# A recurrent head's output read by two engines, a weight piece behind the turned keys, mask rows on the weight queue

## The chip, the core and the metric

The kernel runs on one core of a Trainium2 chip. The metric is the device time of one execution in microseconds: 2011.34 us is the median of three runs before the change, which lay between 2010.67 and 2016.43 us.

## The reference

One inference step of a two-layer encoder. Its tokens are 16 meta tokens and 512 prompt frames of a new stream, and 8 running streams of 16 frames: 656 in all. Each layer mixes tokens in two head groups side by side, eight heads of latent attention and four recurrent heads (HGRN2), and then has a gated channel mixer. The change touches the recurrent heads and the start of the attention behind them:

```python
def hgrn_chunk(S, q, gl, k, v):
    G = jnp.cumsum(gl, axis=1)
    o_inter = jnp.einsum('bthk,bhkv->bthv', q * jnp.exp(G), S)
    A = jnp.einsum('bthk,btshk,bshk->bhts', q, decay, k)
    o = o_inter + jnp.einsum('bhts,bshv->bthv', A, v)
    S_new = jnp.exp(G_last)[..., None] * S + jnp.einsum('bshk,bshv->bhkv', k * jnp.exp(G_last[:, None] - G), v)
    return S_new, o
...
    o = rmsnorm(o, gain) * jax.nn.silu(hg.astype(f32).reshape(B, T, HG_HEADS, HG_DV))
```

## The kernel before

All data lies with features on the partitions and the 656 tokens along the row. Each engine has one program, written out in order; semaphores tie them together. Weights come as 512 KB pieces of 128 x 1024 numbers. SP loads piece g into one of two raw buffers (`wraw`) once piece g - 2 is split; ACT rounds it to its high part (`whi`, in `w_high`), DVE takes the rest (`wlo`, in `w_low`), and TensorE multiplies with both. SP's loop over the pieces issues them strictly in this order, with other transfers between them at fixed places.

The four recurrent heads of a layer run one after the other (`for h in range(HG)` on each engine). TensorE fills the gaps of head h with the input tiles of the next head, or, in the last head, with the query tiles of the attention (`fill`). Within a head:

- Eight levels (`level`, DVE's `hg_diff`, `hg_decayed`, `hg_take`, ACT's `exp_level`) build the masked products A of queries and keys, with two banks of the PSUM tensor WA in turn.
- `turns`: TensorE turns the values into WA and the keys into WB. ACT copies them to `vtok`, `Z` and `ktok`. Before that ACT has the gates of the next head, then one `w_high`.
- `state_sums`: TensorE multiplies turned keys and values. DVE then builds the running states `st` from WA (`state`), and `dec`.
- `head_out`: TensorE makes the head's output in WA, 512 prompt columns in the first bank, 16 meta and 128 sample columns in the second, and signals `o`.
- ACT squares the output for its norm (`sq`), and DVE multiplies it by gain and gate into `ob` and signals `o_taken`. POOL multiplies the old state S by `dec` (`decay_state`). `new_state` and `finish` on DVE come within the next head.
- TensorE waits for `o_taken` before level 0 of the next head, which writes into WA again; behind the last head it waits for it before `keys(0)`.

Behind the last head of a layer come the key tiles (`keys(0)` to `keys(3)`, copied by ACT to KT in `take_keys`), the sum of squares of the last head, and the first scores (`prompt_scores(l, 0)`). These need three transfers, the mask rows: `kpe` copied to rows 64 to 96 of KT for eight heads (528 KB), and four rows each for KT and Y. They wait for `o` and `dec` of the last head, since KT and Y overlay what that head still reads.

In the profile L420 is TensorE's `mm`, L424 its transposes, L950 ACT's `activation`, L1416 DVE's helper, L364 POOL's `decay_state`, L371 POOL's sum of a rotated query tile (`add_rotated`), L331 the load of a weight piece; L1147, L1149, L1150 are the mask rows and L1151 the state's way out.

## Time and profile before

| | us |
|---|---|
| median of three runs | 2011.34 |
| lowest and highest run | 2010.67, 2016.43 |
| the profiled execution | 2010.24 |
| its span in the trace | 2008.4 |
| TensorE busy in it | 1902.1 |
| DVE busy | 1129.7 |
| ACT busy | 761.2 |
| POOL busy | 115.4 |

The span runs from the first to the last instruction of the trace. Busy times overlap, so only the engine that others wait for counts. Views of the trace name an instruction as out<-in with the kernel's own tensor names, with the idle time before it and what ended that idle time. The granted clock of TensorE is given as a share of 2.4 GHz: 1.00 in most stretches and 0.5, that is 1.2 GHz, in some.

### The profile page before, as it was taken

What the parts mean: (1) busy time and instruction counts of PE and PEld (TensorE: products, weight loads), DVE (VectorE), ACT (ScalarE), POOL (GpSimd) and SP (SyncE); (2) the same over time, 40 slices, a digit from 0 to 9 for tenths busy, and PEclk for the clock granted to TensorE, in tenths of its full rate; (3) what the DMA queues carried; (4) which work ended last, traced back from release to release, by engine and by line L of the source; (5) the groups of instructions that cost most, each with busy time, mean ns of one, the idle gap of its engine ahead of it and who ended that gap; (6) DMA issues with size and microseconds to landing.
All of it is one profiled execution on the core that took longest, in us unless ns stands there. A gap on an engine that the chain in (4) does not pass through costs nothing.

```text
span 2008.4 us, 30210 instructions
## 1 busy us (share of the span) xinstructions
PE 1902.1 (95%) x12028; PEld 1741.8 (87%) x12028; DVE 1129.7 (56%) x1807; ACT 761.2 (38%) x1207; POOL 115.4 (6%) x117
## 2 busy tenths in 40 slices
PE   7999989999999999999999998899999999999996
PEld 6988875579899999999888898655889999999994
DVE  5677775534776316663467778544257662366535
ACT  5434545434432222223453444454354222222235
POOL 0000033300000000000000001332000000000000
PEclk9999999999999999999999999899999999999998
DMA  5111121222121222222121111204112222222211
GB/s 185 66 55 55 65 61 38 78 85 74 51 85 69 76 72 74 74 74 74 55 97 44 55 63 54 85 3 139 57 53 67 77 71 75 73 74 74 74 64 58
DMA packets 45116, 141.82 MB, mean 71 GB/s; under 512 B 5472, under 2 KB 11488, under 8 KB 44960
## 3 DMA queue, kind: packets, MB, share of 16 engines
q1 hardware_dynamic: 36704, 120.20, 17.3%
q10 hardware_dynamic: 8272, 19.69, 3.0%
q8 instruction: 96, 1.57, 0.3%
q14 instruction: 44, 0.36, 0.1%
HBM read 130.13 MB, written 8.65 MB: 69 GB/s over the span
## 4 chain that ended last, share of the span: by engine, by line
PE 72%; DVE 14%; ACT 10%; issue 2%; ACTq 1%; DMA 1%; DVEq 0%; SPq 0%
PE G L420 60%; PE WA L420 7%; PE WB L420 3%; DVE wlo L1416 2%; DVE tmp L1416 2%; DVE Y L1416 1%; ACT Y L950 1%; ACT sq L950 1%; DVE DE L1416 1%; ACT whi L950 1%; PE G L424 1%; DVE X L1416 1%; PE WB L424 1%; DVE Z L1416 1%; ACT Hh L950 1%
## 5 line engine op out<-in xcount | busy, mean ns | idle before, releaser
L420 PE MATMUL G<-Hh,wlo 128*128 128x328 f32 x2144 | 690.5, 322 | 30.4 <-DVE Hl L1416 27.6
L420 PE MATMUL G<-Hh,whi 128*128 128x328 f32 x2144 | 675.6, 315 | 0.0
L420 PE MATMUL G<-Hl,whi 128*128 128x328 f32 x2144 | 670.0, 312 | 0.0
L420 PEld LDWEIGHTS G<-Hh,wlo 128*128 128x128 f32 x2144 | 407.4, 190 | 46.6 <-DVE Hl L1416 32.7
L420 PEld LDWEIGHTS G<-Hh,whi 128*128 128x128 f32 x2144 | 406.9, 190 | 1.6 <-issue 0.2
L420 PEld LDWEIGHTS G<-Hl,whi 128*128 128x128 f32 x2144 | 406.7, 190 | 0.0
L950 ACT ACTIVATE whi<-wraw 128x1024 fp32r<-128x1024 f32 x192 | 203.6, 1060 | 515.6 <-PE G L420 490.9
L1416 DVE TENSOR_TENSOR wlo<-wraw,whi 128x1024 fp32r<-128x1024 f32 x192 | 236.4, 1231 | 237.5 <-ACT whi L950 227.6
L420 PE MATMUL G<-gl,whi 128*128 128x328 f32 x704 | 220.4, 313 | 0.0
L420 PE MATMUL G<-gh,wlo 128*128 128x328 f32 x704 | 220.2, 313 | 0.0
L420 PE MATMUL G<-gh,whi 128*128 128x328 f32 x704 | 219.6, 312 | 0.0
L420 PEld LDWEIGHTS G<-gh,whi 128*128 128x128 f32 x704 | 132.2, 188 | 0.2
L420 PEld LDWEIGHTS G<-gh,wlo 128*128 128x128 f32 x704 | 132.2, 188 | 0.2
L420 PEld LDWEIGHTS G<-gl,whi 128*128 128x128 f32 x704 | 132.2, 188 | 0.0
L1416 DVE TENSOR_TENSOR ax<-G,R 128x328 f32<-128x328 f32 (+2 forms) x126 | 48.6, 386 | 136.5 <-PE G L420 133.2
L950 ACT ACTIVATE tmp<-cc 128x528 f32<-128x528 f32 x88 | 42.3, 480 | 145.3 <-DVE cc L1416 143.9
L420 PEld LDWEIGHTS WA<-Z 128*128 128x128 f32 x576 | 71.6, 196 | 27.3 <-DVE Z L1416 16.6
L420 PE MATMUL WA<-Z 128*128 128x64 f32 (+1 forms) x576 | 73.3, 274 | 18.5 <-DVE Z L1416 10.5
L1416 DVE SCALAR_TENSOR_TENSOR cc<-ax,cols,cc 128x672 f32<-128x672 f32 x88 | 80.9, 919 | 3.1
L364 POOL TENSOR_TENSOR S<-S,dec 128x1024 f32<-128x1024 f32 x8 | 15.2, 1897 | 1039.5 <-PE WA L420 1039.3
L950 ACT ACTIVATE DE<-DE 128x512 f32<-128x512 f32 (+1 forms) x64 | 45.3, 708 | 66.3 <-DVE DE L1416 62.8
L1416 DVE TENSOR_TENSOR DE<-Y 128x328 f32<-128x328 f32 (+4 forms) x136 | 61.7, 454 | 5.1
(243 smaller groups left out, 2429.5 us busy)
## 6 DMA issues: line engine op xcount, KB each, us to landing
wraw<-in_wstream SPq DMA_DIRECT2D x192, 512.0 KB, 3.2
ckT<-in_ckT SPq DMA_DIRECT2D x12, 512.0 KB, 3.9
ctok<-in_ctok SPq DMA_DIRECT2D x12, 512.0 KB, 3.3
S<-in_s ACTq DMA_DIRECT2D x8, 512.0 KB, 6.0
o_sst<-S ACTq DMA_DIRECT2D x8, 512.0 KB, 3.1
o_y<-Y SPq DMA_DIRECT2D x16, 164.0 KB, 1.8
ckT<-in_ckT ACTq DMA_DIRECT2D x4, 512.0 KB, 3.9
ctok<-in_ctok ACTq DMA_DIRECT2D x4, 512.0 KB, 3.8
```

What stands on the lines that cost most here:

```text
L364: pool.tensor_tensor(s3, s3, dec[:, :].rearrange("p (b a) -> p b a", a=1).broadcast_to([P, DB, P]), ALU.mult).then_inc(S("s0_decayed"), 1)
L420: return pe.matmul(out, lhsT, rhs, start=start, stop=stop, skip_group_check=True)
L424: return pe.transpose(out, in_, ident[0:n, 0:n])
L950: return act.activation(*args, **kw)
L1416: return kind(*args, **kw)
```

## The change

Three edits, in both layers:

1. In each head, ACT's `w_high` of the piece that stood before the copy of the turned values now stands behind that of the turned keys, and DVE's `w_low` of this piece stands behind `dec` instead of before the state updates.
2. ACT squares the 512 prompt columns of the output and signals `sq_prompt`; meanwhile DVE multiplies the 16 and 128 columns of the second bank and signals `ob_side`. Then ACT squares these, and DVE multiplies the 512. Before, DVE's three products waited for all three squares. TensorE waits for the last squares on its own before `keys(0)`.
3. The three mask-row transfers move from ACT's queue to SP's, just before weight piece 26 of the layer (`P_OUT + 4`), with the same two waits.

```diff
--- before.py
+++ after.py
@@ -326,6 +326,15 @@
                             latents(l, b + 1)
                         sp.wait_ge(S("s_oa"), l * DB + b - 1)
                         sp.dma_start(ctok[:, b % 2, :], a["ctok"][l, b]).then_inc(S(f"ct_in{b % 2}"), 16)
+                if g % PIECES == P_OUT + 4:
+
+                    l = g // PIECES
+                    sp.wait_ge(S("o"), HG * (l + 1))
+                    sp.wait_ge(S("dec"), HG * (l + 1))
+                    sp.dma_start(KT[64:96, :, :], kpe[64:96, 0:PT].rearrange("p (a n) -> p a n", a=1)
+                                 .broadcast_to([ROPE, HM, PT])).then_inc(S("maskrows"), 16)
+                    sp.dma_start(KT[96:100, :, :], a["krows"]).then_inc(S("maskrows"), 16)
+                    sp.dma_start(Y[96:100, :, :], a["qrows"]).then_inc(S("maskrows"), 16)
                 if g >= RAW:
                     sp.wait_ge(S("w_split"), g - RAW + 1)
                 sp.dma_start(wraw[:, g % RAW, :], a["wstream"][g // PIECES, stored(g % PIECES)])\
@@ -824,6 +833,7 @@
                     mm(WB[0:P if i < 4 else META, c:c + 512], kvn[:, cs], wA[:, 512:1024]).then_inc(S("values"), 1)
 
                 pe.wait_ge(S("o_taken"), l * HG + HG)
+                pe.wait_ge(S("sq"), squares(n0 + N_HG[HG - 1]) + 1)
                 keys(0)
                 keys(1)
                 pe.wait_ge(S("s0_new"), l * HG + HG)
@@ -1122,11 +1132,9 @@
                     did(f(DE[:, 0, :], DE[:, 0, :], ACT.Exp), "E")
                     if not end:
                         gates(h + 1)
-                        w_high(l, SPL + 8 + 4 * h)
                     else:
                         for q in range(HG):
                             q_nope(q)
-                        w_high(l, SPL + P_UQ)
                     act.wait_ge(S("v_turned"), n + 1)
                     did(f(vtok[:, 0:640], WA[:, 0:640], ACT.Copy), "act")
                     did(f(vtok[0:META, 640:768], WA[0:META, 640:768], ACT.Copy), "act")
@@ -1136,23 +1144,19 @@
                     act.wait_ge(S("k_turned"), n + 1)
                     did(f(ktok[:, 0:640], WB[:, 0:640], ACT.Copy), "act")
                     did(f(ktok[0:META, 640:768], WB[0:META, 640:768], ACT.Copy), "tok")
+                    w_high(l, SPL + 8 + 4 * h if not end else SPL + P_UQ)
                     if not end:
                         exp_level(h + 1, 0)
                     else:
                         q_nope(4)
                         q_nope(5)
                     act.wait_ge(S("o"), n + 1)
-                    if end:
-                        act.wait_ge(S("dec"), n + 1)
-                        act.dma_start(KT[64:96, :, :], kpe[64:96, 0:PT].rearrange("p (a n) -> p a n", a=1)
-                                      .broadcast_to([ROPE, HM, PT])).then_inc(S("maskrows"), 16)
-                        act.dma_start(KT[96:100, :, :], a["krows"]).then_inc(S("maskrows"), 16)
-                        act.dma_start(Y[96:100, :, :], a["qrows"]).then_inc(S("maskrows"), 16)
                     act.dma_start(a["o_pst"][l, h], st[:, 4, :]).then_inc(S("pst_out"), 16)
                     c = squares(n0 + N_HG[h])
                     if c >= 2:
                         act.wait_ge(S(sq_free(c)[0]), sq_free(c)[1])
-                    did(f(sq[:, c % 2, META:PT], WA[:, 0:512], ACT.Square), "act")
+                    did(f(sq[:, c % 2, META:PT], WA[:, 0:512], ACT.Square), "sq_prompt")
+                    act.wait_ge(S("ob_side"), n + 1)
                     did(f(sq[:, c % 2, 0:META], WA[:, 512:512 + META], ACT.Square), "act")
                     did(f(sq[:, c % 2, PT:T], WA[:, 640:640 + SAMP], ACT.Square), "sq")
 
@@ -1617,7 +1621,7 @@
                     did(tt_(ob[:, h, :], ob[:, h, :], R2[:, :], ALU.mult), "ob")
                     did(mark(), "R2_used")
 
-                def take_tile(h, u):
+                def take_tile(h, u, split=True):
 
                     i = 6 + 4 * h + u
                     to = (hq(h + 1), gate[:, (h + 1) % 2, :], hv(h), hk(h))[u] if i < T_LAT else \
@@ -1630,7 +1634,8 @@
                         did(mark(), "R_used")
                     else:
                         scaled(t0 + i, to)
-                    w_low(l, SPL + i)
+                    if split:
+                        w_low(l, SPL + i)
 
                 gated(0)
                 hg_diff(l, 0, 0)
@@ -1686,11 +1691,10 @@
                         gated(h + 1)
                         hg_diff(l, h + 1, 0)
                         dve.wait_ge(S("v_turned"), n + 1)
-                        take_tile(h, 2)
+                        take_tile(h, 2, False)
                     else:
                         queries(2)
                         queries(3)
-                        w_low(l, SPL + P_UQ)
 
                     dve.wait_ge(S("dS"), n + 1)
                     if n:
@@ -1703,19 +1707,21 @@
                     if n:
                         dve.wait_ge(S("s0_decayed"), n)
                     did(cp(dec[:, :].rearrange("p (b a) -> p b a", a=1), samples(DE[:, 1, PT:T])[:, :, DT - 1:DT]), "dec")
+                    w_low(l, SPL + 8 + 4 * h if not end else SPL + P_UQ)
                     if not end:
                         hg_decayed(l, h + 1, 0)
                     else:
                         queries(4)
                         queries(5)
 
-                    c = squares(n0 + N_HG[h])
+                    def gated_out(to, src):
+                        return stt(ob[:, h, to], src, col(l, C_HGN), gate[:, h % 2, to], ALU.mult, ALU.mult)
+
                     dve.wait_ge(S("o"), n + 1)
-                    dve.wait_ge(S("sq"), c + 1)
-                    gt = gate[:, h % 2, :]
-                    for (p0, p1), (a0, a1) in (((0, 512), (META, PT)), ((512, 512 + META), (0, META))):
-                        step(stt(ob[:, h, a0:a1], WA[:, p0:p1], col(l, C_HGN), gt[:, a0:a1], ALU.mult, ALU.mult))
-                    did(stt(ob[:, h, PT:T], WA[:, 640:640 + SAMP], col(l, C_HGN), gt[:, PT:T], ALU.mult, ALU.mult), "o_taken")
+                    step(gated_out(slice(0, META), WA[:, 512:512 + META]))
+                    did(gated_out(slice(PT, T), WA[:, 640:640 + SAMP]), "ob_side")
+                    dve.wait_ge(S("sq_prompt"), n + 1)
+                    did(gated_out(slice(META, PT), WA[:, 0:512]), "o_taken")
                 queries(6)
                 new_state(HG - 1)
                 queries(7)
```

How the order moves on the engines. In the rows below, an instruction stands with what it writes and reads and the semaphores that it waits for.

DVE in head 0 of layer 0, from the differences of the next head to the output, before:

```order
L1416 TENSOR_TENSOR DE<-Y 128x4x64 [waits dve] x2
L1416 TENSOR_TENSOR Y<-G,R 128x656 [waits D,tile,v_turned]
L1416 TENSOR_TENSOR wlo<-wraw,whi 128x1024 [waits evac0,w_hi]
L1416 COPY st<-WA 128x128 [waits w_split,dS]
L1416 SCALAR_TENSOR_TENSOR st<-st,DE,WA 128x128 [waits state] x4
L1416 COPY dec<-DE 128x8 [waits state]
L1416 TENSOR_TENSOR Z<-Y,DE 128x4x64 [waits dec,E]
L1416 TENSOR_TENSOR Z<-Y,DE 128x4x64 [waits dve]
L1416 SCALAR_TENSOR_TENSOR ob<-WA,cols,gate 128x512 [waits Z,sq,o]
L1416 SCALAR_TENSOR_TENSOR ob<-WA,cols,gate 128x16 [waits dve]
L1416 SCALAR_TENSOR_TENSOR ob<-WA,cols,gate 128x128 [waits dve]
```

and now:

```order
L1420 TENSOR_TENSOR DE<-Y 128x4x64 [waits dve] x2
L1420 TENSOR_TENSOR Y<-G,R 128x656 [waits D,tile,v_turned]
L1420 COPY st<-WA 128x128 [waits evac0,dS]
L1420 SCALAR_TENSOR_TENSOR st<-st,DE,WA 128x128 [waits state] x4
L1420 COPY dec<-DE 128x8 [waits state]
L1420 TENSOR_TENSOR wlo<-wraw,whi 128x1024 [waits dec,w_hi]
L1420 TENSOR_TENSOR Z<-Y,DE 128x4x64 [waits w_split,E]
L1420 TENSOR_TENSOR Z<-Y,DE 128x4x64 [waits dve]
L1420 SCALAR_TENSOR_TENSOR ob<-WA,cols,gate 128x16 [waits Z,o]
L1420 SCALAR_TENSOR_TENSOR ob<-WA,cols,gate 128x128 [waits dve]
L1420 SCALAR_TENSOR_TENSOR ob<-WA,cols,gate 128x512 [waits ob_side,sq_prompt]
```

The low part of the piece (wlo) has moved from before the copy to st to behind dec, and the products ob now begin with the short ones, which no longer wait for `sq`.

ACT in the last head of layer 0, from the turned values to the squares, before:

```order
L950 ACTIVATE whi<-wraw 128x1024 [waits q_nope,tile,w_in1]
L950 ACTIVATE vtok<-WA 128x640 [waits w_hi,v_turned]
...
L950 ACTIVATE ktok<-WB 128x640 [waits tok,k_turned]
L950 ACTIVATE ktok<-WB 16x128 [waits act]
...
L1147 DMA KT<-kpe 32x8x528 [waits dec,o]
L1149 DMA KT<-in_krows 4x4224
L1150 DMA Y<-in_qrows 4x5248
L1151 DMA o_pst<-st 128x128
L950 ACTIVATE sq<-WA 128x512 [waits q_nope,sq_summed]
L950 ACTIVATE sq<-WA 128x16 [waits act]
L950 ACTIVATE sq<-WA 128x128 [waits act]
```

and now:

```order
L960 ACTIVATE vtok<-WA 128x640 [waits q_nope,v_turned]
L960 ACTIVATE vtok<-WA 16x128 [waits act]
L960 ACTIVATE Z<-WA,ind 128x128 [waits act] x2
L960 ACTIVATE ktok<-WB 128x640 [waits tok,k_turned]
L960 ACTIVATE ktok<-WB 16x128 [waits act]
L960 ACTIVATE whi<-wraw 128x1024 [waits tok,tile,w_in1]
...
L1154 DMA o_pst<-st 128x128 [waits o]
L960 ACTIVATE sq<-WA 128x512 [waits q_nope,sq_summed]
L960 ACTIVATE sq<-WA 128x16 [waits sq_prompt,ob_side]
L960 ACTIVATE sq<-WA 128x128 [waits act]
```

The piece's high part (whi) stands behind ktok, the three mask-row transfers are gone, and the second square waits for `ob_side`.

## Rows read from the trace of the kernel before

**Rows 1.** The page: its first line, and part 1, the engines' busy time.
```profile
span 2008.4 us, 30210 instructions
...
PE 1902.1 (95%) x12028; PEld 1741.8 (87%) x12028; DVE 1129.7 (56%) x1807; ACT 761.2 (38%) x1207; POOL 115.4 (6%) x117
```

**Rows 2.** Who TensorE waited for, whole span: us in total, times, longest us.
```profile
PE WA L420 <- DVE ob L1416: 11.8, 8, 3.1
...
PE WB L420 <- ACT ktok L950: 9.0, 6, 1.5
```

**Rows 3.** Order of time, layer 0, head 0, turned keys: start us, us, engine, line, instruction [idle].
```profile
103.44 0.82 PE L424 MATMUL WA<-ident,Y 128*128 128x128 f32 x6
...
104.11 1.06 ACT L950 ACTIVATE whi<-wraw 128x1024 fp32r<-128x1024 f32 x1
...
105.26 1.00 ACT L950 ACTIVATE vtok<-WA 128x640 f32<-128x640 f32 x2
...
108.21 0.70 PE L420 MATMUL WB<-Z,ktok 32*128 32x256 f32 x4 [1.50 <-ACT ktok L950]
```

**Rows 4.** The same view, layer 0, head 0, from the output to the next head.
```profile
117.33 1.04 PE L420 MATMUL WA<-Y,S 128*128 128x16 f32 x8
...
118.56 1.90 POOL L364 TENSOR_TENSOR S<-S,dec 128x1024 f32<-128x1024 f32 x1 [117.73 <-PE WA L420]
...
118.82 1.12 ACT L950 ACTIVATE sq<-WA 128x512 f32<-128x512 f32 x3 [9.94 <-PE WA L420]
...
120.03 1.41 DVE L1416 SCALAR_TENSOR_TENSOR ob<-WA,cols,gate 128x512 f32<-128x512 f32 x3 [5.91 <-ACT sq L950]
...
121.58 1.08 PE L420 MATMUL WA<-Z 128*128 128x64 f32 x8 [1.30 <-DVE ob L1416]
```

**Rows 5.** The page, part 5: DVE's low parts of the weight pieces.
```profile
L1416 DVE TENSOR_TENSOR wlo<-wraw,whi 128x1024 fp32r<-128x1024 f32 x192 | 236.4, 1231 | 237.5 <-ACT whi L950 227.6
```

**Rows 6.** Squares and products of the output: duration ns min/median/max, first and last start, forms.
```profile
L950 ACT ACTIVATE sq<-WA x24: 183/277/600, 118.8 to 1270.6; 128x512 f32<-128x512 f32 x8, 128x16 f32<-128x16 f32 x8, 128x128 f32<-128x128 f32 x8
...
L1416 DVE SCALAR_TENSOR_TENSOR ob<-WA,cols,gate x24: 233/351/753, 120.0 to 1272.0; 128x512 f32<-128x512 f32 x8, 128x16 f32<-128x16 f32 x8, 128x128 f32<-128x128 f32 x8
```

**Rows 7.** Who TensorE waited for, 280:310, end of the heads in layer 0.
```profile
PE WA L420 <- DVE ob L1416: 1.5, 1, 1.5
PE G L420 <- DVE Y L1416: 1.1, 2, 0.6
```

**Rows 8.** Who TensorE waited for, 1262:1295, the same place in layer 1.
```profile
PE WA L420 <- DVE ob L1416: 3.1, 1, 3.1
...
PE G L420 <- DVE Y L1416: 0.6, 1, 0.6
```

**Rows 9.** Order of time, layer 1, last head, to the first scores.
```profile
1256.27 1.56 POOL L371 TENSOR_TENSOR Y<-Y,tmp 32x656 f32<-32x656 f32 x1 [0.24 <-DVE Y L1416]
...
1256.58 2.33 DVE L1416 TENSOR_TENSOR wlo<-wraw,whi 128x1024 fp32r<-128x1024 f32 x1 [0.46 <-DVE Y L1416]
...
1261.22 0.49 PE L420 MATMUL WA<-Am,vtok 128*128 128x128 f32 x2 [0.44 <-DVE st L1416]
...
1265.73 0.70 ACTq L1147 DMA_DIRECT2D KT<-kpe  x1
...
1274.28 1.38 PEld L420 LDWEIGHTS G<-kvn,wA 128*128 128x128 f32 x4 [1.06 <-DVE Y L1416]
...
1278.91 0.87 PE L420 MATMUL G<-KT,Y 100*128 100x144 f32 x4
```

**Rows 10.** Order of time, layer 0: the second key tile.
```profile
292.77 1.16 PE L420 MATMUL G<-kvn,wA 128*128 128x264 f32 x4 [0.64 <-DVE Y L1416]
```

**Rows 11.** Stretches: us, PE, PEld, DVE, ACT, POOL busy, PE clock, DMA share, GB/s.
```profile
1270.00:1272.00 2.00, 0.00 (x0) 0.00 (x0) 0.98 (x2) 1.75 (x5) 0.00 (x0) 1.00 0.57 106
1272.00:1274.00 2.00, 1.13 (x4) 0.68 (x4) 1.81 (x3) 0.79 (x2) 0.00 (x0) 1.00 0.14 13
...
1294.00:1316.00 22.00, 20.90 (x87) 13.97 (x88) 6.18 (x20) 6.30 (x16) 5.71 (x8) 0.53 0.17 60
```

## The prediction

> **What bounds the kernel now.** I read the page first. TensorE is busy for 95% of a span of 2008.4 us, and every other engine for far less [rows 1]: only time in which TensorE waits, or runs slowly, can be won. The second view is who TensorE waited for. Two of its entries belong to the recurrent heads [rows 2]: 11.8 us in 8 waits until DVE has read a head's output ("DVE ob"), one per head, and 9.0 us in 6 waits of 1.5 us at most until ACT has copied the turned keys ("ACT ktok"), in heads 0 to 2 of both layers. The third view, the order of time in head 0 of layer 0, shows how each wait comes about.
>
> At the turned keys [rows 3] TensorE ends the value turns at 103.44 + 0.82 = 104.26. ACT could copy them then, but spends 104.11 to 105.17 on a weight piece (whi), starts vtok at 105.26 and ktok after it, and TensorE, which needs both, starts at 108.21 after 1.50 us of idling.
>
> At the output [rows 4] TensorE's last product ends at 117.33 + 1.04 = 118.37. ACT squares it in three instructions, done at 119.94; DVE, which has stood idle for 5.91 us, reads it in three more from 120.03 to 121.44; TensorE starts the next head's level 0 at 121.58 after 1.30 us of idling. The two engines read one after the other.
>
> **Part 1, the weight piece behind the turned keys, heads 0 to 2.** vtok can start at 104.26 plus the usual 0.07, so at 104.33 instead of 105.26: 0.93 us earlier, and ktok with it. That is less than the 1.50 us that TensorE idles, so it arrives whole. Six such heads: 6 x 0.93 = **5.6 us**. On ACT the piece now stands ahead of the next head's first exponential, and ACT idles long after that. On DVE the low part (1.23 us [rows 5]) moves behind the state updates and dec. There it delays only the next head's Z, and the 5.91 us that DVE idles before ob [rows 4] hide it; without that cover it would cost 1.23 us a head. With this piece no longer ahead of it DVE is free when the state sums end, now also 0.9 us earlier. The piece's split ends later by the state updates, and SP fetches the piece two further on later by as much. The piece itself is first used by the second tile that fills the next head, behind that head's level 3. I cost this at nothing.
>
> **Part 2, the output read by two engines.** The three squares take 0.600, 0.183 and 0.277 us, the three products 0.753, 0.233 and 0.351 [rows 6]. In the new order DVE does its two short ones on the second bank while ACT does its long one (118.82 to 119.42). DVE's long one then runs from 119.51 to 120.26, beside ACT's two short ones. TensorE can start at about 120.4 instead of 121.58. It reaches this place at 121.58 - 1.30 = 120.28, so some 0.1 us of waiting is left: 1.18 us less for TensorE. DVE's own next work starts 1.0 to 1.2 us earlier too, and TensorE's later waits in the head are on that. The eight waits are 11.8 us [rows 2], the two of the last heads 1.5 [rows 7] and 3.1 us [rows 8], so the six of heads 0 to 2 are 7.2 us, 1.2 us each. With 0.1 us left in each, and 0.05 us for the engines' meeting of the next paragraph, I take 6 x 1.05 = **6.3 us**. A new wait stands in ACT's queue (its short squares wait for DVE's short products), but in heads 0 to 2 DVE is idle when the output comes.
>
> DVE's next differences now start at about 120.28, when POOL's decay of the state (118.56 + 1.90) still runs for 0.18 us [rows 4]. The rows of layer 1 show what such a meeting can cost: the low part at 1256.58 took 2.33 us instead of 1.23, and POOL's sum beside it ended 1.25 us after it began [rows 9]. The Trainium skill, page "SBUF — State Buffer", section "Who interferes with whom", says that a DVE instruction with two SBUF inputs and a GpSimd instruction that reads SBUF exclude each other, and the later one waits whole. The trace agrees with it in those rows. By it part 2 would be up to 6 x 0.18 = 1.1 us smaller than without a meeting.
>
> **Part 3, the last head of each layer.** Here the three mask-row transfers also leave ACT's queue. In layer 1 they are issued from 1265.73 on [rows 9], right when the output is ready, and ACT squares only behind the four issues. In the new kernel ACT issues one transfer, squares, and is done before TensorE has finished the last two query tiles. DVE must first do query tiles 4 and 5, now behind the weight piece, so ACT's short squares wait for DVE; the weight piece's 1.23 us is less than the 3.1 us that TensorE idled here, so that too ends before TensorE is through. So the ob waits of 1.5 us in layer 0 [rows 7] and 3.1 us in layer 1 [rows 8] go. Behind them stood waits on DVE's query tiles 6 and 7 (1.1 and 0.6 us), which shrink since these tiles no longer stand behind ob; the sum of squares and the third key tile may find a new short one, for which I leave 0.1 and 0.2 us. Layer 0: 1.5 + 1.1 - 0.1 = **2.5 us**. Layer 1: 3.1 + 0.6 - 0.2 = 3.5 us. Two things are added in layer 1. The second key tile took 2.13 us there [rows 9] against 1.16 us in layer 0 [rows 10], at half clock right after the 3.1 us of idling; I expect it at full clock, 0.97 us. And DVE's first state update no longer stands behind the 2.33 us piece, which ended the 0.44 us wait before head_out [rows 9]. Layer 1: 3.5 + 1.0 + 0.4 = **4.9 us**.
>
> **Part 4, the mask rows on SP.** The price is their landing. In the last head of layer 1 the output came at 1265.7, and the traffic of these rows ends before 1272 [rows 11]: 6.3 us. Scores need them. They started at 1278.91 [rows 9], 13.2 us after the output; with 4.5 us taken out that is 8.7 us. So 2.4 us of cover are left. On SP the rows stand behind weight piece 25, which is now asked for only behind dec, about when head_out starts (1261.22 [rows 9], 4.5 us before the output); nothing is due behind them, since the next piece waits for a split that comes later. The lower bound of their cost is nothing, the upper bound is that they land 4 us later than now, 1.6 us a layer. I take nothing, as the same bytes go over the same engines.
>
> **The sum.** 5.6 + 6.3 + 2.5 + 4.9 = 19.3 us, against a profiled execution of 2010.24 us (1.84 us more than its span). The median of the runs shown is 2011.34 us, 1.1 us above it. From the median: **1992.0 us**.
>
> **The rivals.**
> 1. *Part of it comes back (2001 us).* The heads are a chain over four engines. If the gain at ob is met by the next Z wait, and the key gain by the state wait, about half arrives: 19.3 - 10 = 9.3 us. For it: DVE is busy nearly all through a head. Against it: the DVE chain starts from ob and moves with it, and so does ACT's chain up to the keys. Chance 0.15.
> 2. *Mask rows as the new wait.* If they land at 10.7 us after the output instead of 6.3, TensorE waits 2 us a layer: 1996 us. It ends slower than before if they land later than 8.7 + 9.65 = 18.3 us after the output in each layer, for example at 22 us: 2018 or 2019 us. This would need SP's queue to be held by the weight piece ahead of them. Against it is that this piece's condition, dec, comes before the output. Chance 0.05, of which 0.02 for the slow end.
> 3. *The clock does more (1982 us).* In layer 1's attention the granted clock averaged 0.53 over 22 us [rows 11], so some 20.7 us at 1.2 GHz, which lengthened that stretch by up to 10.3 us. If this stretch stays at 2.4 GHz with everything shifted, 1992 - 10.3 = 1982 us. The Trainium skill, page "TensorE: Matmul & The Clock Gate", section "What's actually happening", says that the lower clock is what idling leads to and that activity releases it. By this rule less idling gives fewer slow stretches, but the waits in the attention stay. Chance 0.08. The other way round, a slow stretch of this length elsewhere would cost 10.3 us: 2002 us, chance 0.02.
> 4. *The change does nothing* because another engine sets the pace: page and waits speak against it. Chance 0.02.
>
> **How the numbers follow.** The forecast of 1992 us has 0.68. The range 1983 to 2001 us takes in the part-way rival, late mask rows and most of the clock's gain; about 0.15 is left outside. About 6 us, or 0.3%, is what a measurement can tell from no change. Faster by more: 0.68 + 0.15 + 0.03 + 0.08 + 0.02 = 0.96. Within: 0.02. Slower: 0.02.
>
> **What would show it.** The ktok waits fall from 1.5 to about 0.6 us in six heads. The eight ob waits fall from 11.8 us to under 1.5 us. In the last heads ob's last instruction ends before TensorE's last query product. No wait on mask rows stands before the first scores, less than 9 us after the output. DVE idles about 4 us, not 5.9, before its first ob. I am wrong if the ktok or ob waits turn up again under "DVE Z", "DVE st" or "DVE S", if scores wait for a transfer, or if the sum of the waits falls by 18 us and the span does not, in which case the clock is to be read.

## The result and the profile after

The changed kernel ran in 1988.78 us (median of 4 runs, 1978.08 to 1994.18), against 2013.88 us (4 runs, 2010.67 to 2018.53) before: a ratio of 0.9871, with a 95% interval of 0.9838 to 0.9903. Two later measurements, each beside new runs of the kernel before, gave 0.9838 (0.9800 to 0.9875) and 0.9850 (0.9827 to 0.9872). The kernel is 1.3 to 1.6% faster. 1992.0 us was forecast, in a range of 1983 to 2001.

The runs of one kernel lie 4 to 26 us apart, and most of this goes with TensorE's clock. Over 56 later runs of the kernel before, the mean granted clock lay between 0.969 and 0.983, and a run was 1.62 us shorter for each 0.001 that it was higher (a line fitted through them; the runs lie about 2 us off it). So beside each time the table in the next section gives the mean clock, and the span times the clock, which takes most of the clock's part out.

The page of the changed kernel, first line and part 1, the lines that answer to [rows 1]:

```profile
span 1985.7 us, 30228 instructions
...
PE 1896.6 (96%) x12028; PEld 1738.2 (88%) x12028; DVE 1129.3 (57%) x1807; ACT 761.1 (38%) x1207; POOL 114.4 (6%) x117
```

Who TensorE waited for (us in total, times, longest us). These answer to [rows 2]:

```profile
PE G L429 <- DVE Y L1420: 4.6, 5, 1.8
...
PE WB L429 <- ACT ktok L960: 3.2, 6, 0.5
PE G L429 <- DMA Y<-in_qrows: 3.0, 2, 1.6
...
PE WB L429 <- DVE S L1420: 0.4, 2, 0.2
```

The wait on the turned keys is down from 9.0 to 3.2 us, 0.5 us in each of the same six heads. The wait on ob, 11.8 us before, is gone from the list altogether. There is a new one on a transfer: two waits on the query rows, one in each layer, 3.0 us together.

In order of time, head 0 of layer 0, from the turns to the next head's level 0. It answers to [rows 3] and [rows 4]:

```profile
101.97 0.81 PE L433 MATMUL WA<-ident,Y 128*128 128x128 f32 x6
...
102.82 1.00 ACT L960 ACTIVATE vtok<-WA 128x640 f32<-128x640 f32 x2 [0.30 <-PE WA L433]
...
105.77 0.70 PE L429 MATMUL WB<-Z,ktok 32*128 32x256 f32 x4 [0.53 <-ACT ktok L960]
105.83 1.06 ACT L960 ACTIVATE whi<-wraw 128x1024 fp32r<-128x1024 f32 x1
...
110.41 1.23 DVE L1420 TENSOR_TENSOR wlo<-wraw,whi 128x1024 fp32r<-128x1024 f32 x1
...
112.78 1.86 PE L429 MATMUL WA<-Y,S 128*128 128x16 f32 x16
...
114.68 0.62 DVE L1420 SCALAR_TENSOR_TENSOR ob<-WA,cols,gate 128x16 f32<-128x16 f32 x2 [1.69 <-PE WA L429]
...
115.08 1.18 ACT L960 ACTIVATE sq<-WA 128x512 f32<-128x512 f32 x3 [7.47 <-PE WA L429]
...
115.71 0.75 DVE L1420 SCALAR_TENSOR_TENSOR ob<-WA,cols,gate 128x512 f32<-128x512 f32 x1 [0.41 <-ACT sq L960]
```

The copy of the turned values starts 0.04 us after the turns end (102.78) and not a microsecond later; the weight piece (whi) follows at 105.83, behind ktok, and its low part at 110.41, behind dec. At the output, which is ready at 112.78 + 1.86 = 114.64, DVE starts at once with its two short products, and the long one runs from 115.71, beside ACT's short squares (the ACT line at 115.08 holds all three squares, the long one first). It ends at 116.46, 1.82 us after the output, where before the last product ended 3.07 us after it.

The last head of layer 1, which answers to [rows 9]:

```profile
1243.95 1.86 PE L429 MATMUL WA<-Y,S 128*128 128x16 f32 x16
...
1245.83 0.60 SPq L334 DMA_DIRECT2D KT<-kpe  x1
1245.84 0.34 ACTq L1154 DMA_DIRECT2D o_pst<-st  x1
...
1246.28 0.60 ACT L960 ACTIVATE sq<-WA 128x512 f32<-128x512 f32 x1 [4.20 <-PE WA L429]
...
1246.69 1.48 DVE L1420 SCALAR_TENSOR_TENSOR ob<-WA,cols,gate 128x16 f32<-128x16 f32 x3
...
1247.02 1.63 SPq L337 DMA_DIRECT2D Y<-in_qrows  x1
...
1249.36 1.05 PE L429 MATMUL WA<-kvn,wA 128*128 128x264 f32 x4
...
1256.24 0.97 PE L429 MATMUL G<-KT,Y 100*128 100x144 f32 x4 [1.43 <-DMA Y<-in_qrows]
```

ACT issues one transfer and squares 0.44 us later, SP issues the mask rows beside it. The products end at 1248.17, 1.2 us before TensorE is through with its queries and starts the first key tile. But the first scores, at 1256.24, have waited 1.43 us for the query rows: 10.4 us after the output, not the 8.7 us that was forecast.

### The profile page after: what moved, and what is told of

Its sections match the earlier page's. It is cut to its first block, busy times and chain, and to the rows that moved or that the text cites. A ratio compares the mean times of both kernels' runs of the same rounds, so it can differ in the third digit from the quotient of the medians.

```text
span 1985.7 us, 30228 instructions
## 1 busy us (share of the span) xinstructions
PE 1896.6 (96%) x12028; PEld 1738.2 (88%) x12028; DVE 1129.3 (57%) x1807; ACT 761.1 (38%) x1207; POOL 114.4 (6%) x117
## 4 chain that ended last, share of the span: by engine, by line
PE 77%; DVE 12%; ACT 7%; DMA 2%; issue 2%; ACTq 0%; SPq 0%; DVEq 0%
PE G L429 63%; PE WA L429 8%; PE WB L429 3%; DVE wlo L1420 2%; DVE tmp L1420 2%; ACT sq L960 1%; DVE X L1420 1%; PE G L433 1%; PE WB L433 1%; DVE Y L1420 1%; ACT whi L960 1%; ACT Hh L960 1%; DVE Z L1420 1%; DVE Hl L1420 1%; DMA Y<-in_qrows 1%
```

## The experiments

All kernels were timed beside new runs of the kernel before. "Clock" is the mean granted clock over the kernel's runs, "span x clock" the median over them. The three measurements of the kernel before gave 1964.9, 1965.8 and 1965.0 for it (28, 11 and 17 runs). e1, e2, e3 and e11 ran 11 or 12 times, the others 5 or 6 times. The single runs of one kernel scatter by 1 to 4 us (standard deviation) in this product, so a median of six is good to about 1.5 us, and a difference of two such medians to about 2 us.

| kernel | median us | ratio | 95% interval | clock | span x clock |
|---|---|---|---|---|---|
| before | 2013 to 2018 | 1 | | 0.9755 | 1965 |
| e1, keys part alone | 1999.81 | 0.9929 | 0.9905 to 0.9952 | 0.9808 | 1960.0 |
| e2, output part alone | 2009.42 | 0.9965 | 0.9935 to 0.9994 | 0.9772 | 1959.8 |
| e3, mask rows alone | 2007.03 | 0.9968 | 0.9942 to 0.9994 | 0.9791 | 1962.2 |
| e4, keys and output | 1987.16 | 0.9875 | 0.9843 to 0.9906 | 0.9840 | 1951.2 |
| e5, the changed kernel | 1985.20 | 0.9838 | 0.9800 to 0.9875 | 0.984 | 1953.6 |
| e6, query rows first | 1987.59 | 0.9854 | 0.9811 to 0.9897 | 0.9820 | 1951.0 |
| e7, query rows on ACT | 1982.00 | 0.9822 | 0.9789 to 0.9856 | 0.9850 | 1950.9 |
| e8, without query rows | 1979.12 | 0.9810 | 0.9773 to 0.9848 | 0.9853 | 1947.9 |
| e9, the changed kernel | 1989.07 | 0.9850 | 0.9827 to 0.9872 | 0.984 | 1953.5 |
| e10, output and mask rows | 1997.38 | 0.9893 | 0.9858 to 0.9927 | 0.9818 | 1959.7 |
| e11, ACT's half of keys | 2008.87 | 0.9953 | 0.9933 to 0.9973 | 0.9817 | 1970.7 |
| e12, mask rows early | 1977.21 | 0.9790 | 0.9770 to 0.9810 | 0.9868 | 1949.7 |

The clock of e5 and e9 is the mean over the 15 runs of the changed kernel. A second table helps with the last heads. It gives, from each kernel's order of time, the us from the end of the last head's output on TensorE to the first key tile, from there to the first scores, and the sum, for layer 0 and layer 1.

| kernel | to key tile | to scores | sum |
|---|---|---|---|
| before | 6.74, 6.81 | 5.97, 6.40 | 12.71, 13.21 |
| e1 | 6.76, 6.72 | 5.97, 5.97 | 12.73, 12.69 |
| e2 | 5.66, 5.51 | 6.35, 6.36 | 12.01, 11.87 |
| e3 | 3.56, 3.56 | 7.01, 6.90 | 10.57, 10.46 |
| e4 | 5.63, 5.63 | 6.35, 6.36 | 11.98, 11.99 |
| changed | 3.53, 3.55 | 7.04, 6.88 | 10.57, 10.43 |
| changed, e5 | 3.56, 5.08 | 6.96, 5.46 | 10.52, 10.54 |
| changed, e9 | 3.56, 5.07 | 7.02, 5.48 | 10.58, 10.55 |
| e6 | 3.56, 5.09 | 6.16, 4.86 | 9.72, 9.95 |
| e7 | 3.53, 3.53 | 6.59, 6.54 | 10.12, 10.07 |
| e8 | 3.56, 3.53 | 5.28, 5.31 | 8.84, 8.84 |
| e12 | 5.06, 5.09 | 4.71, 4.85 | 9.77, 9.94 |

### The three parts, each alone

**e1, the keys part alone.** All that the diff moves of ACT's `w_high` and DVE's `w_low`, and nothing else. The main lines:

```diff
                         gates(h + 1)
-                        w_high(l, SPL + 8 + 4 * h)
...
+                    w_high(l, SPL + 8 + 4 * h if not end else SPL + P_UQ)
                     if not end:
                         exp_level(h + 1, 0)
...
-                        take_tile(h, 2)
+                        take_tile(h, 2, False)
...
+                    w_low(l, SPL + 8 + 4 * h if not end else SPL + P_UQ)
```

> Only the weight piece moves behind the turned keys (ACT's high part and DVE's low part); the output is still read in turn and the mask rows stay on ACT. Theory (the terms add up): the six ktok waits fall from 1.5 to about 0.5 us, 5.8 us in all; the eight ob waits stay near 11.8 us; layer 1's wait on DVE st (0.4 us) goes. The span times its granted clock falls by 5 to 7 us. Rival (one chain, the gain comes back at the next wait): ob, Z or state waits grow by several us and the same product falls by less than 3 us.

```profile
PE WA L420 <- DVE ob L1415: 13.3, 8, 3.0
PE WA L420 <- DVE Z L1415: 9.8, 11, 1.8
...
PE WB L420 <- ACT ktok L950: 3.1, 6, 0.5
```

The ktok waits fell by 5.9 us, to 0.5 us each, and the wait on st is gone. Z did not take them over (9.8 us against 10.5 before the change); ob rose a little, from 11.8 to 13.3 us. Span x clock fell by 4.9 us, just under the bound of 5. The theory that the terms add up holds. The time fell by more, 0.7%, and the clock was higher too (0.9808 against 0.976 beside it).

**e2, the output part alone.** The `sq_prompt` and `ob_side` hunks and TensorE's extra wait:

```diff
+                pe.wait_ge(S("sq"), squares(n0 + N_HG[HG - 1]) + 1)
                 keys(0)
...
-                    did(f(sq[:, c % 2, META:PT], WA[:, 0:512], ACT.Square), "act")
+                    did(f(sq[:, c % 2, META:PT], WA[:, 0:512], ACT.Square), "sq_prompt")
+                    act.wait_ge(S("ob_side"), n + 1)
...
+                    step(gated_out(slice(0, META), WA[:, 512:512 + META]))
+                    did(gated_out(slice(PT, T), WA[:, 640:640 + SAMP]), "ob_side")
+                    dve.wait_ge(S("sq_prompt"), n + 1)
+                    did(gated_out(slice(META, PT), WA[:, 0:512]), "o_taken")
```

> Only the output is read by two engines; the weight piece stands before the turned values and the mask rows stay on ACT. Theory: the six ob waits of heads 0 to 2 vanish (7.2 us); in the last heads ACT still squares behind four transfer issues, but the long product no longer waits for the short squares, so of 4.6 us of waiting about half stays. ktok waits stay at 9.0 us. Span times clock falls by 8 to 10 us. Rival (DVE's chain gives it back at Z): the Z waits grow from 10.5 us by more than 4 us.

```profile
PE WA L420 <- DVE Z L1418: 10.6, 13, 1.8
PE WB L420 <- ACT ktok L951: 9.0, 6, 1.5
...
PE G L420 <- DVE Y L1418: 8.0, 8, 1.8
...
PE WA L420 <- DVE ob L1418: 3.7, 2, 2.0
```

The six waits of heads 0 to 2 vanished; the two that are left, 3.7 us, are those of the last heads. Z stayed at 10.6 us, so the rival falls. But span x clock fell by 5.1 us and not by 8 to 10. The expectation had counted 7.2 + 2.3 us. The ob waits did fall by 8.1 us, but 1.3 us came back as waits on DVE's query tiles (DVE Y 8.0 us, before 6.7), and in the last head of layer 0 the scores start only 0.7 us sooner after the output (second table). All of TensorE's waits on DVE, ACT and transfers fell by some 7 us, 2 us more than the product; that is about the size of the scatter, and what it is otherwise is not shown.

**e3, the mask rows alone.** The SP block of the diff in and ACT's three transfers out, nothing else.

> Only the mask rows move to SP's queue. Theory: in the last heads ACT squares about 4 us earlier, the ob waits of 1.5 and 3.1 us go, the other six stay at 7.2 us, and the first scores start about 2 to 4 us earlier in each layer with a wait on the query rows of 0 to 1 us, since they land about 10.3 us after the output whatever the queue. Span times clock falls by 3 to 5 us. Rival (the transfer on SP lands later than on ACT because it stands behind a weight piece): the first scores start no earlier, the product stays.

```profile
PE WA L429 <- DVE ob L1419: 7.0, 6, 1.4
...
PE G L429 <- DMA Y<-in_qrows: 2.3, 2, 1.2
```

Both ob waits of the last heads went; the six others stayed. The scores start 10.5 us after the output instead of 12.7 and 13.2, and wait 2.3 us for the query rows, 1.1 to 1.2 us in each layer and so a little more than the 0 to 1 us expected. Span x clock fell by 2.7 us, a little short of the 3 to 5 expected; the direction is clear, and the rival (no earlier scores) falls.

The three products of span and clock add up: 4.9 + 5.1 + 2.7 = 12.7 us, against 1965 - 1953 = 12 us for the whole change, which is agreement within the scatter.

**e4, both other parts, with the mask rows on ACT.**

> Both other parts, with the mask rows still on ACT. Theory: ktok and ob waits of heads 0 to 2 as in the changed kernel; in the last heads ob waits come back (1 to 3 us in each layer) because ACT issues four transfers before it squares, and the mask rows land about as long after the output as on SP. The span times clock lies 1 to 4 us above that of the changed kernel. Rival (SP is the worse queue): no wait on mask rows, and the product equals or beats the changed kernel's.

```profile
PE G L420 <- DVE Y L1417: 8.0, 8, 1.8
...
PE WB L420 <- ACT ktok L951: 3.2, 6, 0.5
...
PE WA L420 <- DVE ob L1417: 2.3, 2, 1.9
```

ob waits came back (2.3 us in all), and the scores start 1.4 to 1.5 us later than in the changed kernel, as the theory has it. Yet span x clock is 1951.2, not above 1953.5: over 6 runs each the two can't be told apart, and neither can their times. Counted in TensorE's order of time, moving the mask rows is worth some 1.5 us a layer behind the other two parts; in the measured time of the whole it does not show. Which of two prices it has (0 or 3 us) is left open by e4.

**e10, the changed kernel without the keys part.**

> The changed kernel without part 1: the weight piece stands before the turned values again. Theory (the lower clock goes with idling at the keys): ktok waits are back at 9.0 us, span times clock is about 5 us above the changed kernel's, and the mean granted clock is about 0.977 instead of 0.984, which adds some 13 us more: a time near 2003 us. Rival (the clock's gain is luck of the executions, or comes from any wait removed): the clock stays at 0.982 or more and the time is near 1992 us.

```profile
PE WB L429 <- ACT ktok L960: 9.0, 6, 1.5
```

The ktok waits are back at 9.0 us and span x clock is 6.2 us above the changed kernel's, as forecast. The clock part of the theory fell: it stayed at 0.982 over the six runs, and the time was 1997.4 us, between the two forecasts. So the ktok waits alone do not carry the clock's gain.

**e5 and e9, the changed kernel again**, as the measure for the kernels that ran beside it.

> The changed kernel once more, as the reference for the three beside it. Expected: a ratio of 0.985 to 0.990, span times clock about 1952 us, and a wait of about 1.5 us on the query rows (Y<-in_qrows) before the first scores of each layer.

> The changed kernel as the reference for the three beside it: span times clock 1951 to 1954 us, ratio 0.984 to 0.990.

The tables have what came of them. In both, the wait on the query rows is there again. In layer 1 the last query tiles ran at half clock, so TensorE came to the scores later and waited only 0.4 and 0.5 us there; the scores started 10.5 us after the output all the same.

### The half that was costed at nothing

**e11** moves ACT's high part behind the turned keys and leaves DVE's low part before the state updates. It is e1 without its changes on DVE:

```diff
                         gates(h + 1)
-                        w_high(l, SPL + 8 + 4 * h)
...
+                    w_high(l, SPL + 8 + 4 * h if not end else SPL + P_UQ)
```

> Of part 1 only ACT's half, and neither part 2 nor 3: the high part moves behind the turned keys, DVE's low part stays before the state updates. DVE then waits for the high part, which ends about 2.1 us after ktok does in the changed order, so the low part delays the first state update by about 0.6 us and TensorE's head_out. Theory: ktok waits at 3.1 us as with the whole part 1, but waits on DVE st come up, 0.5 to 1.0 us in each of the six heads, 3 to 6 us in all; span times clock lies 2 to 5 us above that of part 1 alone (1960.0). Rival (DVE's half is free, as my prediction's zero for it says in either place): no wait on st above 1 us in all, the product as with part 1 alone.

```profile
PE WA L420 <- DVE ob L1415: 14.2, 8, 3.1
...
PE WA L420 <- DVE st L1415: 5.7, 8, 1.1
...
PE WB L420 <- ACT ktok L950: 3.3, 6, 0.5
...
PE WA L420 <- DVE Am L1415: 2.6, 2, 1.3
```

The ktok waits are at 3.3 us, and what they gave comes back at once as 5.7 us of waits on st, in all eight heads. With 0.9 us more on ob, 2.6 us on Am and 0.7 us on Y, this makes 9.9 of the 10.7 us by which span x clock lies above e1's; the forecast of 2 to 5 us was too small. By that measure this half alone is 5.7 us slower than the kernel before (1970.7 against 1965). The time itself does not say so: the ratio to the kernel before beside it is 0.9953 (0.9933 to 0.9973), so it was faster, with a mean clock of 0.982 where that kernel had 0.975. Why the clock was higher is not shown. What e11 does show is that DVE's half is no side issue: with the low part left in its place, the waits that the high part's move takes away come back in front of the state updates, and more. (The 2.1 us of the expectation count from ktok's start; in the changed kernel whi ends 1.2 us after ktok ends.)

### The mask rows

**e6, the query rows first.**

```diff
+                    sp.dma_start(Y[96:100, :, :], a["qrows"]).then_inc(S("maskrows"), 16)
+                    sp.dma_start(KT[96:100, :, :], a["krows"]).then_inc(S("maskrows"), 16)
                     sp.dma_start(KT[64:96, :, :], kpe[64:96, 0:PT].rearrange("p (a n) -> p a n", a=1)
                                  .broadcast_to([ROPE, HM, PT])).then_inc(S("maskrows"), 16)
-                    sp.dma_start(KT[96:100, :, :], a["krows"]).then_inc(S("maskrows"), 16)
-                    sp.dma_start(Y[96:100, :, :], a["qrows"]).then_inc(S("maskrows"), 16)
```

> The changed kernel with the three mask-row transfers on SP issued in the order query rows, key rows, kpe. Theory (the query rows are slow by themselves, and land late because they are issued last): issued about 1.3 us earlier, they land before the scores are due; the 528 KB kpe copy then ends last, by the traffic some 7 us after the output, before the 9 us at which scores are due, so the 3.0 us of waiting on transfers before the scores go and span times clock falls by 1 to 3 us. Rival (what costs is all the rows' traffic together, in whatever order): the wait stays at about 3 us, under another transfer's name.

SP's issues in the last head of layer 1 of e6, in order of time:

```profile
1243.91 0.27 SPq L334 DMA_DIRECT2D Y<-in_qrows  x1
...
1244.22 0.30 SPq L335 DMA_DIRECT2D KT<-in_krows  x1
...
1244.56 0.62 SPq L336 DMA_DIRECT2D KT<-kpe  x1
```

The three issues take 0.27, 0.30 and 0.62 us; in the changed order the query rows alone took 1.63 us. The wait on transfers fell to 0.7 us, on kpe and in layer 0 alone. In the second table the scores come 9.72 and 9.95 us after the output, so 0.6 to 0.8 us earlier. So the query rows no longer end last. But the kpe copy, now behind them, does: in layer 0 TensorE waits for it until 9.72 us after the output, where the expectation had it there after some 7 us. The order gains 0.8 of the 1.7 us that leaving the query rows out gains (e8). In layer 1 no wait shows, since TensorE's query tiles ran at half clock and it came to the scores later by itself. Span x clock is 2.6 us lower than e5's in the same measurement, about the size of the scatter, and the times can't be told apart.

A side result says more about these rows. The state's way out (o_pst, 64 KB) is issued by ACT here, on a queue with no mask row ahead of it, beside the query rows on SP. It landed 5.9 and 5.5 us after its issue, in layers 0 and 1, where it took 1.6 us in the changed kernel, which issues it beside the kpe copy.

**e7, the query rows on ACT** ahead of the state's way out, with kpe and key rows on SP.

> The changed kernel with the query rows alone issued by ACT, ahead of the state's way out and the squares, and kpe and key rows on SP. Theory: the query rows start 1.3 us earlier and beside kpe, so the wait of 3.0 us falls below 1 us; ACT's squares start about 1.5 us later, which TensorE does not see because it ends its query tiles later still (ob waits below 0.5 us in all). Rival (two queues at once share the same engines and end no earlier): the wait stays at 2 us or more and an ob wait comes back.

```profile
PE G L428 <- DMA KT<-in_krows: 2.0, 2, 1.1
```

The wait has the key rows' name now and is 2.0 us, and the scores come 10.1 us after the output. No ob wait came back. The rival holds in its main point, a wait of 2 us, but not in the ob wait. The key rows, behind kpe on SP, now end last. When the query rows landed is not shown, but the state's way out behind them on ACT landed 8.0 and 8.4 us after its issue, so small rows are slow on a queue of their own too, with kpe running beside them.

**e8, without the query rows.** The transfer is left out, and TensorE waits for the other two; the causal mask within the blocks is not applied.

> Leaves out the transfer of the query rows, so the causal mask inside the 128-token blocks is not applied; kpe and key rows stay on SP. Theory: no transfer wait stands before the first scores, which start about 1.5 us earlier in each layer, so span times clock lies 2 to 3 us under the changed kernel's: the whole price of part 4. Rival: the key rows or kpe land just as late, and the wait stays under their name.

In the second table the first scores now come 8.84 us after the output in both layers, and no transfer stands before them. Against 10.5 us that is the whole price of part 4: 1.7 us a layer. Span x clock is 5.7 us under e5's, more than the 2 to 3 us expected, by about the scatter.

**e12, the mask rows in two groups.** The query rows of seven heads, and key rows and kpe of four, lie on places that the last head has already left when its sample sums are done:

```diff
-                    sp.wait_ge(S("o"), HG * (l + 1))
                     sp.wait_ge(S("dec"), HG * (l + 1))
-                    sp.dma_start(KT[64:96, :, :], kpe[64:96, 0:PT].rearrange("p (a n) -> p a n", a=1)
-                                 .broadcast_to([ROPE, HM, PT])).then_inc(S("maskrows"), 16)
-                    sp.dma_start(KT[96:100, :, :], a["krows"]).then_inc(S("maskrows"), 16)
-                    sp.dma_start(Y[96:100, :, :], a["qrows"]).then_inc(S("maskrows"), 16)
+                    sp.wait_ge(S("dS_sample"), HG * (l + 1))
+
+                    def rows(h0, h1):
+                        sp.dma_start(Y[96:100, h0:h1, :], a["qrows"][:, h0:h1, :]).then_inc(S("maskrows"), 16)
+
+                    def keyrows(h0, h1):
+                        sp.dma_start(KT[96:100, h0:h1, :], a["krows"][:, h0:h1, :]).then_inc(S("maskrows"), 16)
+                        sp.dma_start(KT[64:96, h0:h1, :], kpe[64:96, 0:PT].rearrange("p (a n) -> p a n", a=1)
+                                     .broadcast_to([ROPE, h1 - h0, PT])).then_inc(S("maskrows"), 16)
+
+                    rows(0, 4)
+                    rows(5, HM)
+                    keyrows(0, 4)
+                    sp.wait_ge(S("o"), HG * (l + 1))
+                    rows(4, 5)
+                    keyrows(4, HM)
...
-                pe.wait_ge(S("maskrows"), 48 * (l + 1))
+                pe.wait_ge(S("maskrows"), 112 * (l + 1))
```

> The changed kernel with the mask rows in two groups on SP, query rows first in each: those whose places are free already (query rows of heads 0 to 3 and 5 to 7, key rows and kpe of heads 0 to 3) as soon as dec and the sample state sums are done, the rest after the output. Theory: half the bytes are under way about 3 us before the output, so no transfer wait stands before the first scores; they start about 1.7 us earlier in each layer, as without the query rows, and span times clock is 2 to 4 us under the changed kernel's. Rival (seven transfers cost more to issue and land than three): the wait stays at 1 us or more a layer, and the product is no lower.

The last head of layer 1 of e12, in order of time:

```profile
1243.54 0.26 SPq L336 DMA_DIRECT2D Y<-in_qrows  x1
...
1244.24 0.59 SPq L340 DMA_DIRECT2D KT<-kpe  x1
...
1248.60 1.05 PE L440 MATMUL WA<-kvn,wA 128*128 128x264 f32 x4
...
1252.46 1.16 PE L440 MATMUL G<-kvn,wA 128*128 128x264 f32 x4 [0.48 <-DVE Y L1431]
...
1253.45 0.87 PE L440 MATMUL G<-KT,Y 100*128 100x144 f32 x4
```

and its clock in single microseconds (us, busy PE, PEld, DVE, ACT, POOL, PE clock, DMA share, GB/s):

```profile
1244.00:1245.00 1.00, 1.00 (x5) 1.00 (x5) 0.85 (x3) 0.58 (x1) 0.73 (x2) 0.50 1.10 157
...
1246.00:1247.00 1.00, 1.00 (x5) 1.00 (x5) 0.00 (x0) 0.26 (x1) 0.92 (x2) 0.50 1.15 150
```

No transfer stands before the scores, which start at once behind the third key tile: 4.71 and 4.85 us behind the first one, the shortest of all kernels. The sum is still 9.8 to 9.9 us and not 8.8, because in this execution the last query tiles ran at 1.2 GHz in both layers (5.1 us to the key tile, else 3.5). So the trace shows that the rows had landed by 9.8 us after the output, and not whether they would have been there at 8.8. e12 has the lowest time of all: 1977.21 us, a ratio of 0.979 (0.977 to 0.981) to the kernel before, with an interval that lies below that of the changed kernel in the same measurement (0.9827 to 0.9872). It overlaps those of e7 and e8. Span x clock is 3.8 us under e9's, within the 2 to 4 us expected. The rest of the 12 us between the medians goes with the clock (0.987 against 0.983 in e9's five runs); that the early rows are what raises it is not shown.

## Why the prediction was right, and where it was not

**Part 1, the keys: right.** 5.6 us were forecast; the waits fell by 5.8 us with the whole change and 5.9 us alone. What was left in each head, 0.57 us by the working, is 0.5 us. DVE's half was rightly placed at nothing, but for more than the reason given: e11 shows that in its old place it would have eaten the gain.

**Part 2, the output in heads 0 to 2: right, a little low.** 6.3 us forecast; all 7.2 us went. The side figure, that DVE would still idle about 4 us before its first product, was wrong: it idles 1.69 us there, and 0.41 us more before the long one. The old 5.91 us lose 1.62 us to the earlier start (114.68, 0.04 us behind the output, where it was 1.66) and 1.23 us to the low part, which makes 3.1. The other 1.3 to 1.4 us are TensorE's, which gets from its first sum over the turned keys to the output in 8.87 us (105.77 to 114.64), where it took 10.16 (108.21 to 118.37). That part is the clock: the tile that it multiplies in between ran at a mean granted clock of 0.57 before (110 to 114 us, where the 1.50 us of idling had ended at 108.21) and at 1.00 now. The half-speed stretch now comes behind the output instead (115 to 119 us, again 0.57). So the cover of the low part is thinner than I had it, though it held. I had left 0.1 us a head and 0.05 us for DVE meeting POOL. DVE's differences at 116.50 took 0.96 us where they took 0.88 before, so the meeting is there, and its price is under 0.1 us. By the section "Who interferes with whom" of the Trainium skill, page "SBUF — State Buffer", the later one waits whole, which here would be until POOL's decay ends at 114.82 + 1.90 = 116.72, so 0.22 us; the row shows 0.08. POOL's spans in a trace are rough, so this is no strong test of the rule. e2 gives 5.1 us for this part, with the last heads in it.

**Part 3, the last heads: right.** The ob waits (1.5 and 3.1 us) went, those on DVE's query tiles fell from 6.7 to 4.6 us in all, and the one on st went. That is 4.6 + 2.1 + 0.4 = 7.1 us, less 0.2 us more on DVE S: 6.9 us, against 6.4 us forecast without the clock's 1.0. That 1.0 us came too: the second key tile of layer 1 takes 1.16 us at full clock. A slip in the rows stood beside this part: the line of 1274.28 shows the weight loads of the second key tile (1.38 us). The 2.13 us of the text is this line of the same view of the kernel before:

```profile
1274.28 2.13 PE L420 MATMUL G<-kvn,wA 128*128 128x264 f32 x4 [0.64 <-DVE Y L1416]
```

**Part 4, the mask rows: wrong, the failed step.** "In the last head of layer 1 the output came at 1265.7, and the traffic of these rows ends before 1272": 6.3 us. The end of the traffic was taken for the landing. The changed kernel has the same gap. Its output in layer 1 comes at 1245.81, and from 1252 to 1253 there is no traffic (us, busy PE, PEld, DVE, ACT, POOL, PE clock, DMA share, GB/s):

```profile
1252.00:1253.00 1.00, 1.00 (x4) 0.48 (x3) 0.97 (x2) 0.97 (x2) 0.10 (x1) 1.00 0.00 0
```

Yet TensorE waits until 1256.24. The rows landed 10.4 to 10.6 us after the output in each layer of the kernel, in e3, e5, e9 and e10 too, whether TensorE came to wait early or late. One line of the kernel before would have warned of it. It is the view of what reads the states, in the last head of layer 1:

```profile
L1151 ACTq DMA_DIRECT2D o_pst<-st x1: 966/966/966, 1268.7 to 1268.7; - x1
...
DMA to landing us min/median/max: 7.6/7.6/7.6
```

This transfer was issued behind the mask rows on the same queue and landed 7.6 us later, at 1276.3, while the same transfer of the other heads needs 1.6 us (the median of all eight). That is 10.6 us after the output, about when the rows land. It is a sign and no proof of what the queue's order does, since in e6 the same transfer took 5.5 to 5.9 us with no row ahead of it on its queue. The prediction had 8.7 us for when the scores would be due, and e8 measures 8.84. So the cover of 2.4 us was in truth a lack of 1.7 us a layer: 3.4 us, of which 3.0 us show as waits. My second rival gave this 1996 us at a landing of 10.7 us and a chance of 0.03. Its landing was what happened, within the rest of the gain. What these small rows spend the last 4 us on, with the traffic over, stays open.

**The sum of the waits.** Forecast 18.3 us (19.3 without the clock's 1.0). With lower-clock time taken out, half of 81.9 us before and half of 67.3 us after, by the windows of one microsecond added up over both traces, the spans are 1967.4 and 1952.0 us: 15.4 us. The difference to the 18.3 us is 2.9 us, the size of part 4. The waits themselves sum to more, 5.8 + 7.2 + 6.9 - 3.0 = 16.9 us; where the other 1.5 us went is not shown.

**The clock: the term that was mis-sized.** I counted 1.0 us for it. In the profiled pair it gave 7.3 us. Over all runs the mean clock went from 0.9755 (56 runs) to 0.984 (15 runs), which at 1.62 us for 0.001 is 13 to 14 us, as much as all the waits. The third rival looked for this gain in layer 1's attention. In the first profiled execution of the changed kernel it is not there. These are that stretch, against the last of [rows 11], and the query tiles behind the last output of layer 1, in the same columns as above:

```profile
1272.00:1293.00 21.00, 19.90 (x81) 13.28 (x79) 5.55 (x20) 5.97 (x14) 5.72 (x8) 0.51 0.19 63
1245.00:1249.00 4.00, 4.00 (x30) 4.00 (x30) 3.21 (x6) 1.77 (x4) 3.65 (x3) 1.00 0.61 144
```

What fell in this pair is the number of short stretches in and around the heads. The trace of before has half-speed time in the query tiles behind the last output of layer 0 and at the second key tile of layer 1; the profiled execution of the change has neither. But in e5, another execution of the same changed kernel, it is the other way round:

```profile
1272.00:1293.00 21.00, 19.75 (x104) 12.18 (x105) 9.56 (x31) 10.85 (x27) 7.49 (x11) 0.92 0.20 64
1245.00:1249.00 4.00, 4.00 (x18) 4.00 (x19) 2.41 (x5) 1.42 (x4) 3.64 (x3) 0.57 0.66 139
```

The long slow stretch of the attention is all but gone, the query tiles run slowly, and the execution took 1978.07 us, 9.5 us less than the first one (1987.55). That is the third rival's mechanism and nearly its time, though in some executions only. In e9, 1994.08 us, a stretch as long stood in layer 0 (305 to 327 us at 0.53) and none in layer 1. So where the clock falls changes from one execution of a kernel to the next, and a single profiled pair can't tell where the change gained. The Trainium skill, page "TensorE: Matmul & The Clock Gate", section "What's actually happening", says that idling leads to the lower clock; the direction agrees, as every part that took idling away raised the mean clock (0.9808, 0.9772 and 0.9791 alone, 0.984 together, against 0.9755). But e10, with all of the 9.0 us ktok waits back, still had 0.982, and e11, with as much waiting as the kernel before, 0.982 as well. Why the mean clock rises stays open; the amount of waiting alone does not order it.

**The time.** Waits of 15 us and a clock's gain of 7 to 14 us make 22 to 29 us. The medians moved by 25 us (2013.88 to 1988.78) and the profiled pair by 22.7 us. The forecast of 19.3 us is too small by the clock's part, less what part 4 took: the two errors have opposite signs. 1992.0 lay 3.2 us above the median and inside the range. Luck had a share in that: it was taken from a median of 2011.34 us that more runs put at 2013 to 2018, which hid 2.5 us of the 5.8 us by which the gain was forecast too small. (The first rival's 2001 us counts from the profiled execution; from the median, as the forecast does, it is 2002, just outside the range.) The mechanisms of parts 1 to 3 were right without luck, since each wait that was named shrank by about what was said.

## What to carry to other kernels

When two engines read one product in turn, and it lies in two banks, let one engine start with the first bank and the other with the second, and then swap: the reader that sets the buffer free here ended after two long instructions one behind the other, instead of six instructions. Look at what an engine does just before a copy that others wait for, and move all of it behind the copy, with the work on other engines that is tied to it (with half of this move, more waiting came back than it took away). Take a transfer's landing from a wait or from a landing time that the profile gives, not from where the traffic stops. Where rows are needed soon, send them earlier: another order or queue gained 0.4 to 0.8 us a layer here, and the early start left no wait in the one trace of it. And do not read the clock's share from one profiled pair.

## What the runs showed of the hardware

- The query rows (82 KB in four rows of 21 KB) landed 10.4 to 10.6 us after the first issue behind a 528 KB copy inside the on-chip memory and the key rows, although the traffic on the queues had all but ended 6 us after it. Put first, they no longer set the end (the copy did, at 9.7 us in layer 0 of e6), and SP issued them in 0.27 us instead of 1.63 us.
- A 64 KB transfer on the other queue landed after 1.6 us beside the 528 KB copy, and after 5.5 to 5.9 us beside the small rows (the changed kernel and e6).
- The time of a run followed the mean granted clock at 1.62 us for 0.001. The clock changed by 0.014 between executions of the kernel before, some 23 us, and by 0.017 between those of e6.
- A stretch of some 20 us of attention at 1.2 GHz was there in one execution of the changed kernel, gone in a second and in the other layer in a third.
- In the last query tiles of layer 1 the clock was full in one execution of the changed kernel and 1.2 GHz in two others (3.55 us against 5.08 and 5.07 us to the key tile), with the same instructions. The waits ahead of them were not the same: in the 21 us up to the output TensorE waited 1.1 us for DVE in the first, and 2.5 us in each of the other two. The first had run at 0.57 for 8 us just before (1221 to 1229 us), the others for 4 us, so it came to DVE's query tiles later. So an early slow stretch may take away the waiting that stands ahead of the next one; three traces suggest it, and no run tested it.
